# Delta rule: the 16-token inverse as 32x32 tiles on the diagonal of the array

## What is computed

```python
def gated_delta_rule_chunked(q, k, v, g, beta):
    ...
    gc = jnp.cumsum(g, axis=-1)
    decay = jnp.where(causal, jnp.exp(jnp.minimum(gc[..., :, None] - gc[..., None, :], 0.0)), 0.0)
    kb = k * beta[..., None]
    m = jnp.where(strict, jnp.einsum('bhnid,bhnjd->bhnij', kb, k) * decay, 0.0)
    eye = jnp.eye(CHUNK, dtype=m.dtype)
    t_inv = lax.linalg.triangular_solve(eye + m, jnp.broadcast_to(eye, m.shape),
                                        left_side=True, lower=True, unit_diagonal=True)
    u = jnp.einsum('bhnij,bhnjd->bhnid', t_inv, v * beta[..., None])
    ...
```

## Time and profile before

| | before |
|---|---|
| median of 3 runs | 3185.23 us (3184.31 to 3192.18) |
| span of the profiled execution | 3188.2 us |
| TensorE busy | 3099.4 us, 97% of the span |
| VectorE busy | 2246.8 us, 70% |
| ScalarE busy | 1742.8 us, 55% |
| GpSimd busy | 821.5 us, 26% |
| TensorE clock granted, mean | 0.990 |

### The profile page before, as it was taken

The page is one execution under the profiler, slowest core; times in us unless marked ns, Lnnn a source line. Parts: engine busy times, 40 slices in busy tenths (PEclk is TensorE's granted clock), DMA queues, the critical chain, the costliest instruction groups (busy, mean ns, idle before and its releaser), DMA issues.

```text
span 3188.2 us, 63691 instructions
## 1 busy us (share of the span) xinstructions
PE 3099.4 (97%) x19926; PEld 2737.0 (86%) x19926; DVE 2246.8 (70%) x4157; ACT 1742.8 (55%) x3855; POOL 821.5 (26%) x1372
## 2 busy tenths in 40 slices
PE   5999999999999999999999999999999999999998
PEld 4999999999978888888888887888888888888887
DVE  5767777777755788667887767886677654776566
ACT  5565666566644555445555556764555544555444
POOL 1000000000010499888888810770000000000000
PEclk8999999999999999999999999999999999999999
DMA  6454444444467777877777766785666677667764
GB/s 166 115 135 123 125 122 132 128 125 122 132 170 190 195 204 208 226 203 203 202 206 208 211 183 166 231 247 153 185 182 186 189 185 185 183 185 185 185 159 142
DMA packets 1036179, 556.43 MB, mean 175 GB/s; under 512 B 38193, under 2 KB 1023953, under 8 KB 1035585
## 3 DMA queue, kind: packets, MB, share of 16 engines
q1 hardware_dynamic: 969088, 491.18, 57.8%
q10 hardware_dynamic: 58160, 37.63, 4.0%
q0 software_dynamic: 8848, 26.59, 2.7%
HBM read 528.30 MB, written 27.03 MB: 174 GB/s over the span
## 4 chain that ended last, share of the span: by engine, by line
PE 73%; DVE 11%; ACT 7%; issue 6%; DMA 1%; ACTq 1%; DVEq 0%; POOL 0%; SPq 0%; POOLq 0%
PE bank L302 39%; PE bank L303 21%; DVE w_lo L286 5%; ACT w_hi L280 3%; PE bank L633 2%; PE bank L299 1%; ACT T L941 1%; PE bank L300 1%; DVE tiles L1935 1%; ACT L941 1%; DVE normed L1947 1%; DVE tiles L328 1%; PE bank L798 1%; ACT dec L941 1%; DVE y L1775 1%
## 5 line engine op out<-in xcount | busy, mean ns | idle before, releaser
L286 DVE TENSOR_TENSOR w_lo<-raw,w_hi 128x512 fp32r<-128x512 f32 x1856 | 1298.1, 752 | 145.2 <-ACT w_hi L280 137.3
L302 PE MATMUL bank<-act,w_hi 128*128 128x512 f32 x3376 | 1227.5, 405 | 17.5 <-DVE w_lo L286 7.8
L303 PE MATMUL bank<-act,w_lo 128*128 128x256 f32 x4352 | 1224.3, 281 | 0.0
L302 PE MATMUL bank<-mid,w_hi 128*128 128x512 f32 x3072 | 1088.1, 399 | 4.1 <-DVE w_lo L286 3.1
L280 ACT ACTIVATE w_hi<-raw 128x512 fp32r<-128x512 f32 x1856 | 1040.9, 620 | 68.7 <-PE bank L303 44.1
L303 PE MATMUL bank<-mid,w_lo 128*128 128x256 f32 x3072 | 860.7, 280 | 0.0
L303 PEld LDWEIGHTS bank<-act,w_lo 128*128 128x128 f32 x4352 | 827.9, 190 | 0.8
L302 PEld LDWEIGHTS bank<-act,w_hi 128*128 128x128 f32 x3376 | 638.1, 189 | 171.9 <-DVE w_lo L286 11.2
L302 PEld LDWEIGHTS bank<-mid,w_hi 128*128 128x128 f32 x3072 | 579.1, 188 | 147.0 <-issue 3.4
L303 PEld LDWEIGHTS bank<-mid,w_lo 128*128 128x128 f32 x3072 | 581.6, 189 | 0.2 <-issue 0.2
L318 ACT ACTIVATE tiles<-bank 128x256 f32<-128x256 f32 x323 | 123.5, 382 | 541.8 <-PE bank L303 535.6
(11 more groups left out here) (331 smaller groups left out, 3122.6 us busy)
## 6 DMA issues: line engine op xcount, KB each, us to landing
raw<-in_mlp_w_up_dram SPq DMA_DIRECT2D x128, 1024.0 KB, 6.6
raw<-in_mlp_w_down_dram SPq DMA_DIRECT2D x128, 1024.0 KB, 6.2
raw<-in_gdn_w_in_dram SPq DMA_DIRECT2D x96, 1024.0 KB, 6.0
raw<-in_gdn_w_out_dram SPq DMA_DIRECT2D x32, 1024.0 KB, 6.8
raw<-in_ple_w_gate_dram SPq DMA_DIRECT2D x32, 1024.0 KB, 6.3
raw<-in_s_w_out_dram SPq DMA_DIRECT2D x28, 1024.0 KB, 6.8
raw<-in_s_w_in_dram ACTq DMA_DIRECT2D x10, 1024.0 KB, 7.1
c_scratch<-c_pow ACTq DMA_DIRECT2D x32, 256.0 KB, 4.6
```

The costliest lines, as they stand in the source:

```text
L286: eng.tensor_tensor(w_lo[par][:, c], raw[slot][:, c], w_hi[par][:, c].bitcast(F32), ALU.subtract).then_inc(S("lo_ready"), 1)
L302: eng.matmul(a[:, :], w_hi[par][:, w], rhs[:, k0 + kt, :], start=(k0 + kt == 0), stop=False)
L303: mm = eng.matmul(a[:, 0:NT], w_lo[par][:, w], rhs[:, k0 + kt, 0:NT], start=False, stop=(k0 + kt == kend - 1))
```

## The change

The 16x16 blocks of one row group of 32 tokens lie inside a 32x32 diagonal block, so everything outside those four 32x32 blocks is zero in slots 0 to 5. The change keeps only the blocks: `pr[:, m, 0, :]` holds the power and `pr[:, m, 1, :]` the inverse, each [128, 4, 32], block j in partitions 32j to 32j+31. `blocks` on TensorE loops over the four row groups j, and in each over the four matrices m, and multiplies a 32x32 block in the part of the array that its rows and its output rows name: 16 products with K = 32 and M = 32 where four with 128 by 128 stood. Square and product with the inverse become one (`first:first + count`, 64 columns). Further:

- the power is turned with VectorE in a 128-element transpose (`spread`, into px0 and px1) and not in one of 512; the third comes out of PSUM directly, so ScalarE has no third copy;
- the merge from 16 to 32 (slot 5) moves from ScalarE to VectorE: one operation with the constant column tcol[:, 2:3] (-1 or 0 by row), then four copies of a block into RT;
- RT must be zero outside its blocks, so GpSimd clears three regions of it for each key head after `kk_done`, and all of it once at the start; VectorE waits for `RT_cleared`;
- ident32 (the identity in 32 columns) and the last 32 rows of WT are set up once on VectorE ahead of the loop;
- ScalarE waits for `mid_lo` in slot 6 and not in slot 0.

```diff
--- before.py
+++ after.py
@@ -158,16 +158,22 @@
         qkn, qkT, dec, Mp, RT, Vb = (gs(n, [P, 4, P]) for n in ("qkn", "qkT", "dec", "Mp", "RT", "Vb"))
         kd, qeT, erow, state = (gs(n, [P, 2, P]) for n in ("kd", "qeT", "erow", "state"))
         gcr = gs("gcr", [P, 4, P])
+        pr = gs("pr", [P, 4, 2, 32])
+        p32, px0, px1, dm32 = (gs(n, [P, 4, 32]) for n in ("p32", "px0", "px1", "dm32"))
+        wt32 = gs("wt32", [P, 4, 16])
+        ident32 = gs("ident32", [P, 32])
         g1.close()
 
-        second_16 = lambda t_, m: t_[:, m, :].rearrange("p (i h q) -> p i h q", i=4, h=2)[:, :, 1, :]
+        block_32 = lambda t_, j: t_[32 * j:32 * j + 32, :, 32 * j:32 * j + 32]
+        pair_of = lambda bk, i: bk[:, 0:256].rearrange("p (m i q) -> p m i q", m=4, i=2)[:, :, i, :]
+
         second_half = lambda t_, m: t_[:, m, :].rearrange("p (i h q) -> p i h q", i=2, h=2)[:, :, 1, :]
         packed = lambda t_, m: t_[:, :, :].rearrange("p m q -> p (m q)")[:, 64 * m:64 * m + 64]
 
...
@@ -625,53 +631,53 @@
                     pe.wait_ge(S("gc_turned_out"), 1)
                     key_products(0)
 
-            def four(bk, lhs, rhs, name, turn_=False):
-                for m in range(4):
-                    if turn_:
-                        mm = pe.transpose(bk[:, m * P:(m + 1) * P], lhs[:, m, :], ident)
-                    else:
-                        mm = pe.matmul(bk[:, m * P:(m + 1) * P], lhs[:, m, :], rhs[:, m, :], start=True, stop=True)
+            def blocks(dst, lhs, rhs, name):
+                pe.sem_inc(S("tiles_begun"), 1)
+                for j in range(4):
+                    for m in range(4):
+                        rows_ = slice(32 * j, 32 * j + 32)
+                        mm = pe.matmul(dst(rows_, m), lhs(rows_, m), rhs(rows_, m), start=True, stop=True)
                 mm.then_inc(S(name), 1)
+
+            def four(bk, power, first, count, name):
+                blocks(lambda rows_, m: bk[rows_, m * 64:m * 64 + 32 * count], lambda rows_, m: power[rows_, m, :],
+                       lambda rows_, m: pr[rows_, m, first:first + count, :].rearrange("p i q -> p (i q)"), name)
 
             def core(r, s):
                 w = lambda name, k=1, o=1: pe.wait_ge(S(name), k * r + o)
                 if s == 0:
                     w("P_ready")
                     w("PT_ready")
-                    four(C, PT, Pm, "power_done")
+                    four(C, p32, 0, 1, "power_done")
                 elif s == 1:
-                    w("power_out", 3, 1)
                     w("RT_ready", 7, 1)
-                    four(A, P2, RT, "R_done")
-                    w("transposed_out", 2, 1)
-                    four(C, P2T, P2, "power_done")
+                    w("power_out", 2, 1)
+                    w("spread_out", 3, 1)
+                    four(A, px0, 0, 2, "power_done")
                 elif s == 2:
-                    w("power_out", 3, 2)
                     w("RT_ready", 7, 2)
-                    four(A, P4, RT, "R_done")
-                    w("transposed_out", 2, 2)
-                    four(C, P4T, P4, "power_done")
+                    w("power_out", 2, 2)
+                    w("spread_out", 3, 2)
+                    four(C, px1, 0, 2, "power_done")
                     w("o_normed")
                     for b in range(2):
                         mm = pe.matmul(B[:, b * P:(b + 1) * P], kq[:, 1, b, :], kq[:, 0, b, :], start=True, stop=True)
                     mm.then_inc(S("qk_done"), 1)
                 elif s == 3:
-                    w("power_out", 3, 3)
                     w("RT_ready", 7, 3)
-                    four(A, P8, RT, "R_done")
+                    w("spread_out", 3, 3)
+                    four(A, px0, 1, 1, "R_done")
                     w("o_log")
                     pe.transpose(E[:, 0:P], kq[:, 1, 0, :], ident).then_inc(S("kv_turned"), 1)
                 elif s == 4:
                     w("RT_ready", 7, 4)
-                    for m in range(4):
-                        mm = pe.matmul(A[0:112, 64 * m:64 * m + 64], Mp[:, m, 0:112], second_16(RT, m), start=True, stop=True)
-                    mm.then_inc(S("X_done"), 1)
+                    blocks(lambda rows_, m: A[rows_, 16 * m:16 * m + 16], lambda rows_, m: Mp[rows_, m, rows_],
+                           lambda rows_, m: pr[rows_, m, 1, 16:32], "X_done")
                 elif s == 5:
                     w("Dm_ready", 3, 1)
                     w("WT_ready", 3, 1)
-                    for m in range(4):
-                        mm = pe.matmul(C[0:112, 64 * m:64 * m + 64], Dm[:, m, 0:112], packed(WT, m), start=True, stop=True)
-                    mm.then_inc(S("R_done"), 1)
+                    blocks(lambda rows_, m: C[rows_, 16 * m:16 * m + 16], lambda rows_, m: dm32[rows_, m, :],
+                           lambda rows_, m: wt32[rows_, m, :], "R_done")
...
@@ -1078,18 +1084,14 @@
             def core(r, s):
                 w = lambda name, k=1, o=1: se.wait_ge(S(name), k * r + o)
                 col = lambda c: hs[:, c:c + 1]
-                by_16 = lambda a: a[:, 0:NT].rearrange("p (m j q) -> p m j q", m=4, j=4)
                 by_half = lambda a: a[:, 0:NT].rearrange("p (m j q) -> p m j q", m=4, j=2)
                 if s == 0:
-                    w("mid_lo")
+                    w("RT_ready", 7, 1)
                     w("power_done", 3, 1)
-                    A_(fl(P2), C[:, :]).then_inc(S("power_out"), 1)
+                    A_(pr[:, :, 0, :], pair_of(C, 0)).then_inc(S("power_out"), 1)
                 elif s == 1:
                     w("power_done", 3, 2)
-                    A_(fl(P4), C[:, :]).then_inc(S("power_out"), 1)
-                elif s == 2:
-                    w("power_done", 3, 3)
-                    A_(fl(P8), C[:, :]).then_inc(S("power_out"), 1)
+                    A_(pr[:, :, 0, :], pair_of(A, 0)).then_inc(S("power_out"), 1)
                 elif s == 3:
...
                 elif s == 4:
                     w("X_done", 3, 1)
-                    A_(fl(WT)[0:112, 0:NT], A[0:112, 0:NT]).then_inc(S("WT_ready"), 1)
-                elif s == 5:
-                    w("R_done", 6, 4)
-                    for j in range(4):
-                        mm = A_(RT[32 * j:32 * j + 16, :, 32 * j + 16:32 * j + 32], by_16(C)[32 * j:32 * j + 16, :, j, :], scale=-1.0)
-                    mm.then_inc(S("RT_ready"), 1)
+                    A_(fl(wt32), A[:, 0:64]).then_inc(S("WT_ready"), 1)
                 elif s == 6:
+                    w("mid_lo")
                     w("X_done", 3, 2)
                     A_(fl(WT)[0:96, 0:NT], A[0:96, 0:NT]).then_inc(S("WT_ready"), 1)
...
@@ -1425,11 +1423,18 @@
             assert len(side) == SIDE_PARAMS
             for dst, src in side:
                 gp.dma_start(dst, src, allow_slow_non_contiguous=dst.shape[-1] == 1).then_inc(S("side_in"), 16)
+            gp.memset(RT[:, :, :].rearrange("p m q -> p (m q)"), 0.0).then_inc(S("RT_cleared"), 1)
...
+            with gp.Fori(1, KH) as r:
+                gp.wait_ge(S("kk_done"), r + 1)
+                gp.sem_inc(S("RT_read"), 1)
+                gp.memset(RT[0:32, :, 32:64], 0.0).then_inc(S("RT_cleared"), 1)
+                gp.memset(RT[64:96, :, 96:128], 0.0).then_inc(S("RT_cleared"), 1)
+                gp.memset(RT[0:64, :, 64:128], 0.0).then_inc(S("RT_cleared"), 1)
...
@@ -1749,6 +1754,7 @@
             link(last)
             ve.wait_ge(S("x_turned"), 16)
             link(ve.memset(pre[:, :, 0:4], 0.0))
+            link(ve.memset(WT[96:128, :, :].rearrange("p m q -> p (m q)"), 0.0))
 
             link(TS(onorm[:, :], onorm[:, :], 0.5 * 128 ** -0.5, None, ALU.mult))
 
@@ -1804,12 +1810,20 @@
                                ALU.mult, ALU.mult)
                 last.then_inc(S("M_ready"), 1)
                 ve.wait_ge(S("M_ready"), r + 1)
-                TT(Pm[:, :, :], Mp[:, :, :], M16N.unsqueeze(1).to_broadcast([P, 4, P]), ALU.mult).then_inc(S("P_ready"), 1)
+                for j in range(4):
+                    at = slice(32 * j, 32 * j + 32)
+                    last = TT(p32[at], block_32(Mp, j), M16N[at, at].unsqueeze(1).to_broadcast([32, 4, 32]), ALU.mult)
+                last.then_inc(S("P_ready"), 1)
                 ve.wait_ge(S("P_ready"), r + 1)
-                ve.transpose(fl(PT), fl(Pm)).then_inc(S("PT_ready"), 1)
+                ve.transpose(pr[:, :, 0, :], p32[:, :, :]).then_inc(S("PT_ready"), 1)
                 ve.wait_ge(S("PT_ready"), r + 1)
-                TT(RT[:, :, :], PT[:, :, :], ident.unsqueeze(1).to_broadcast([P, 4, P]), ALU.add).then_inc(S("RT_ready"), 1)
-
+                TT(pr[:, :, 1, :], pr[:, :, 0, :], ident32[:, :].unsqueeze(1).to_broadcast([P, 4, 32]),
+                   ALU.add).then_inc(S("RT_ready"), 1)
+
+            link(TT(ident32[:, :], ident[:, 0:32], ident[:, 32:64], ALU.add))
+            link(TT(ident32[:, :], ident32[:, :], ident[:, 64:96], ALU.add))
+            link(TT(ident32[:, :], ident32[:, :], ident[:, 96:128], ALU.add))
```

(41 more changed lines are left out.)

10 lines of the change are left out of this document (5 added, 5 removed).

## The result

The changed kernel takes 3206.11 us (median of 8 runs, 3193.11 to 3210.68), the kernel before 3186.10 beside it (8 runs, 3176.76 to 3192.18): a ratio of 1.0057, 95% interval 1.0039 to 1.0075. It is slower by 0.6%, where I forecast 0.15% faster. The time lies inside the wide range of 3167 to 3211, but in the part of it that was there for the slower rivals.

A forecast was written before the change was run, and what follows sets the result against it. TensorE, busy 97% of the span, was taken as the kernel's clock. 16 x (0.46 - 0.10) = 5.8 us less and 0.9 more for setup gave 4.9 us off: 3180 us, own range 3169 to 3193, wide range 3167 to 3211.

The forecast's parts named there:

- wide range: Whole kernel: 3167 to 3211 us, to hold the forecast case, half overlap and the cheaper half of the serial case; 0.82.
- slower rivals: TensorE's `blocks` groups: tiles overlapping only by half, 3195 us, chance 0.12, or serial tiles, 3210 us, chance 0.20.
- eight deep works as four deep did: `blocks` groups on TensorE: tiles run side by side with eight records each; 64 columns 0.63 us, 32 or 16 columns 0.42.
- half overlap rival: `blocks` groups: next tile starts when four records of one are left; 64-column groups 1.1 us, kernel 3195; chance 0.12.
- serial case: `blocks` groups: a record goes out only when the one before left its tile; groups 0.96 and 1.87 us, 3210; chance 0.20.
- signs of being wrong: Slot 6 starting later than 19.3 us after the key matrix's first operation, or groups far from 0.7 us.
- 0.91 us that I held against L786: TensorE: least time for eight 128-column records one behind the other, 6 x 0.106 + 0.27; the row says 0.64.
- my sum: TensorE's 64-column groups: next product 0.63 us after group start, results 0.71 after; 32 or 16 columns 0.42.
- my walk: One head from the key matrix through slot 6: slot 6 0.46 us early, waits 0.9, 0.5 and 1.6 in slots 1, 4, 6.
- order of its waits: TensorE waiting for VectorE: some 0.9 us in slot 1, 0.5 in slot 4, 1.6 ahead of slot 6.
- the clearing: GpSimd clears three RT regions beside two low splits ahead of the key matrix: at most 0.3 us, taken as 0.1 a head.
- Setup: VectorE ahead of the loop: a memset (some 0.3) and three short chained additions (0.2 each), 0.9 us once.

The follow-up runs named there:

- experiment 2: Changed kernel with each group done two matrices at a time, so a tile gets four records in a row, not eight; 3180.36 us, one run.
- experiment 4: Mask tests on experiment 1's kernel: P's four masks on all 128 partitions, 3166.7 us; or three more masks on partitions 0 to 31, 3202.79 us.
- experiment 1: Changed kernel with the four matrices ("heads") looped outside and the row groups inside, two records in a row for a tile; 3188.97 us, ratio to before 1.0014.
- experiment 7: Merge first's kernel, with copies and corners moved to ScalarE, then slot 3's addition and transpose ahead of qk decay, low split and mask; 3134.22 us, ratio 0.9838.
- `same_rows`: Experiment 1's kernel with three more masks, all on partitions 0 to 31, ahead of the four, into tiles that nothing reads; 3202.79 us, one run.
- `spread` first: Experiment 1's kernel with the transpose of the first power ahead of slot 0's low split on VectorE; 3179.54 us, ratio 0.9989.
- 128-partition masks: Experiment 1's kernel with P's four masks on all 128 partitions, each into its own tile, only the last used; 3166.7 us, one run.
- experiment 3: Changed kernel going row group by row group with three matrices, then with the fourth, so a tile gets six records in a row; 3199.52 us, one run.
- merge first: `spread` first's kernel with slot 5's merge, four copies and RT's transpose also ahead of slot 5's low split on VectorE; 3166.51 us, ratio 0.9947.

## Why the prediction was wrong

- **The groups.** "I take it that eight deep works as four deep did": this step failed. The L786 row is right, and experiment 2 repeats it, but it has four records in a row for a tile. Of two neighbours, one four deep and one that went round the tiles, I made a rule for a case that was neither. The half overlap rival was the mechanism, at 0.12, and even there I had 1.1 us and results at 1.25 where it was 1.30 and 1.37; its price, 3195, was 11 us low, and the time is near the 3210 of the serial case, whose mechanism did not occur: its groups were to be 1.87 us long by my estimate, and they are 1.36 to 1.39. That the time lies in my wide range is luck to that extent. Both of my signs of being wrong came true: slot 6 starts 20.38 us after the key matrix for a limit of 19.3, and the groups are far from 0.7 us. (The 0.91 us that I held against L786 has six distances for eight records; with seven it is 1.01, and the row's 0.64 speaks against it all the more.)
- **The sizes.** Each 64-column group brings its result 0.66 later than in my sum, twice on the path: 1.32 us. Slot 1 starts 0.38 late, of which 0.28 are the masks. Together 1.7 at the third power; slot 6 is 1.58 behind my walk (20.38 for 18.8), and the head 1.56 longer than my 51.4.
- **VectorE.** Four masks cost 1.17 for 0.89, since each goes to other partitions (experiment 4). The four copies took 0.91 for 0.85. The order of its waits was right: with quick groups all three came within 0.15 us of the walk (experiment 1), and with slow ones the shorter waits, 0.55, 0.18 and 0.73, are what is left of them.
- **GpSimd.** I took 0.1 us a head for the clearing. Its three memsets (0.19, 0.20 and 0.31 us, from 187.48) lie beside the two low splits ahead of the key matrix, which take 1.29 us together; in the trace of the kernel before the same two take 1.28. It costs nothing that is seen.
- **Setup.** 1.2 us for 0.9, added up from durations: the memset took 0.48 for the 0.3 that I gave it, the three additions 0.23 each from one to the next. It isn't seen as a later start: the loop's first `qkn` starts at 78.26 in the changed kernel's trace and at 79.42 in the other.
- **The forecast without the failed step.** Experiment 1 has the groups that I priced, or slightly quicker ones (0.58 and 0.38 us to the next product for 0.63 and 0.42). Its head is 51.56 for my 51.4, and 51.28 with the masks at my price; the forecast of 3180 was a forecast of that kernel. Beside its own before (3185.24), heads and setup give 3185.24 - 3.7 + 1.2 = 3182.7, and two slowed heads (below) 3 more; measured were 3188.97. The 3 us that are left lie within the interval of the ratio, which begins at 3183.0.
- **The page's rule.** By the Trainium skill, "TensorE: Matmul & The Clock Gate", Part 3, matmuls start and end in program order and a weight load overlaps matmuls of other row groups only. In the changed kernel's trace the second ladder starts 6 ns after the fifth rung of the first, with three records listed ahead of it still to start; read as tiles, that isn't program order. With heads outside, 25 records start in 0.36 us, 14 ns apart on average, so the 25 ns of Part 1 don't hold for these tiles either. That the order of issue matters fits the rule, but here it is the fifth record in a row, not the second, that costs.

## What to carry to other kernels

Small products on different tiles of the array run side by side only if the code lists them so: go round the tiles, and give none more than four fp32 records in a row (shown here for 32x32 tiles and 16 to 64 columns). A row of the trace speaks for the depth, width and order that it has; where the change goes deeper than any row, price it from both ends and let the doubt weigh in the chances. And when a group on one engine gets shorter, look at what the other engine does just ahead of its result: here the gain of 3.4 us a head was held up by three places in VectorE's order and four copies.

## What I had not expected of the hardware

VectorE starts a mask of 32 partitions 0.20 us after one on the same partitions, and 0.29 us after one on others (experiment 4). The four copies into RT, which also go from one partition group to the next, start 0.23 apart and last 0.22. ScalarE does the same in experiment 7: its copies of 32 partitions last 0.31 and start 0.32 apart, while two on all 128 partitions just ahead of them (tile `kd`) last 0.35 and start 0.25 apart.

And TensorE's clock fell in heads with long waits. With three masks more (experiment 4, `same_rows`), every second interval from one `qkn` to the next is 53.70 us, the others 52.15. Stretches of TensorE in that kernel, two whole heads and then the start of slot 6 (207.99) in the second (stretch, length, busy (count), clock, DMA share, GB/s):

```profile
133.08:185.23 52.15, 48.02 (x525) 1.00 0.47 126
185.23:238.93 53.70, 49.56 (x525) 0.97 0.47 122
206.00:210.00 4.00, 2.40 (x17) 0.92 0.16 40
208.00:212.00 4.00, 4.00 (x24) 0.67 0.02 4
210.00:214.00 4.00, 4.00 (x25) 0.65 0.47 123
```

Ahead of the fall TensorE had waited 0.85, 0.94, 0.65 and 1.60 us in slots 0, 1, 4 and 6, with small groups between; then the granted clock was 0.67 and 0.65 over four microseconds each, so for most of the time at the lower of its two levels, 1.2 GHz, and a head costs 1.5 us more. It goes with the waits: with 0.85, 0.94, 0.65 and 1.60 it happens in 7 of 15 intervals, with 0.24, 0.96, 0.65 and 1.60 (heads outside) in 2, with 0.24, 0.35, 0.65 and 1.60 (`spread` first) in one, with 0.96, 0.64 and 1.57 in slots 1, 4 and 6 (128-partition masks) in one, and in none with 0.23, 0.91, 0.62 and 1.51 (experiment 2), with 1.10 or less ahead of slot 6 (the changed kernel, experiment 3, merge first and the versions after it), nor in the kernel before. The waits alone don't decide it: the undisturbed turn from 133.08 has nearly the same ones (0.84, 0.96, 0.65 and 1.58) at a clock of 1.00. No run was made to part the length of the one wait from their sum, and the cause stays open. A faster group whose gain stays a wait can thus lose part of it to the clock.
